# A gated matrix-memory scan on one core: its output gate by ScalarE's sigmoid two steps later instead of by exponential, addition and reciprocal, and the gate's bias added later in a step

## The reference

```
def step(carry, inp):                       # one chunk, one direction
    C, n, m = carry
    ...
    C_new = a[..., None, None] * C + einsum('bhs,bhsd,bhse->bhde', ws, kc, vc)
    w_inter = exp(inter - m_t)
    s = einsum('bhtd,bhsd->bhts', qc, kc) * exp(dmat - m_t[..., None])
    num = w_inter[..., None] * einsum('bhtd,bhde->bhte', qc, C) + einsum('bhts,bhse->bhte', s, vc)
    h = num / maximum(abs(den), exp(-m_t))[..., None]

def mlstm_readout(h, o, norm_g, w_out):     # h: forward plus backward
    hn = h * rsqrt(mean(h * h, axis=-1, keepdims=True) + EPS)
    hn = hn * norm_g
    y = hn * sigmoid(o)                     # o = x @ w_o + b_o, the output gate
    return y @ w_out
```

## Time and profile before

| | |
|---|---|
| median of 3 runs | 3857.44 us (3845.57 to 3867.3) |
| the profiled execution, its own time | 3861.1 us |
| its span | 3859.3 us |
| mean granted clock of TensorE | 0.922 |
| the scan, from step 0's L1890 to the end of the last L1951 | 2622.05 to 2917.89 us, 295.84 us |

### The profile page before, as it was taken

One profiled execution on the slowest core, in us unless ns is written; L12 is line 12 of the kernel. 1 busy time (PEld: TensorE's weight loads), 2 busy tenths in 40 slices (PEclk: granted clock), 3 DMA queues, 4 the chain that ended last, 5 costly groups with the idle time before them and its releaser, 6 DMA issues.

```text
span 3859.3 us, 37214 instructions
## 1 busy us (share of the span) xinstructions
PE 3372.9 (87%) x14970; PEld 2483.2 (64%) x14990; DVE 1545.4 (40%) x2658; ACT 839.0 (22%) x1493; POOL 745.5 (19%) x322
## 2 busy tenths in 40 slices
PE   5986888887789887999999978999977689999998
PEld 2444344444676787888888843447766668888886
DVE  3012788897342136222222334115664633222225
ACT  2013333334312212111111112101222022112111
POOL 2000000000321013332333320001111343223223
PEclk9995888888889988999999988999988889999999
DMA  5100111111112001111111130100002201111112
GB/s 141 41 22 22 55 44 44 44 44 23 55 57 96 28 23 50 44 46 52 43 54 43 44 139 28 44 25 13 13 1 93 93 22 55 44 54 44 47 51 109
DMA packets 173178, 192.25 MB, mean 50 GB/s; under 512 B 24267, under 2 KB 137803, under 8 KB 172284
## 3 DMA queue, kind: packets, MB, share of 16 engines
q1 hardware_dynamic: 163696, 177.20, 14.5%
q10 hardware_dynamic: 9356, 13.31, 1.1%
HBM read 174.71 MB, written 15.78 MB: 49 GB/s over the span
## 4 chain that ended last, share of the span: by engine, by line
PE 58%; issue 16%; DVE 15%; POOL 6%; ACT 3%; DMA 1%; ACTq 1%; POOLq 0%; SPq 0%; DVEq 0%
PE psum L605 9%; PE psum L607 9%; PE psum L606 9%; PE psum L598 7%; PE psum L588 6%; POOL weights_parts L2156 3%; PE psum L970 2%; PE psum L708 2%; DVE x_cols L1592 2%; DVE rows L1590 2%; PE psum L702 2%; POOL region L2204 2%; DVE stats L1510 1%; PE psum L746 1%; PE psum L727 1%
## 5 line engine op out<-in xcount | busy, mean ns | idle before, releaser
L2156 POOL TENSOR_TENSOR weights_parts<-weights,weights_parts 128x2048 fp32r<-128x2048 f32 (+1 forms) x82 | 377.0, 4598 | 986.9 <-ACT weights_parts L1092 986.9
L605 PE MATMUL psum<-x_cols_parts,weights_parts 128*128 128x512 f32 x1344 | 525.7, 391 | 25.6 <-POOL weights_parts L2156 23.9
L607 PE MATMUL psum<-x_cols_parts,weights_parts 128*128 128x512 f32 x1344 | 524.9, 391 | 0.0
L607 PE MATMUL psum<-weights_parts,region_parts 128*128 128x512 f32 (+1 forms) x1120 | 410.3, 366 | 0.0
L605 PE MATMUL psum<-weights_parts,region_parts 128*128 128x512 f32 x864 | 337.5, 391 | 6.9 <-DVE region_parts L2110 5.8
L606 PE MATMUL psum<-weights_parts,region_parts 128*128 128x512 f32 x864 | 337.1, 390 | 0.0
L605 PEld LDWEIGHTS psum<-x_cols_parts,weights_parts 128*128 128x128 f32 x1344 | 253.6, 189 | 79.7 <-issue 24.9
L607 PEld LDWEIGHTS psum<-x_cols_parts,weights_parts 128*128 128x128 f32 x1344 | 253.5, 189 | 53.0
L606 PE MATMUL psum<-x_rows_parts,weights_parts 128*128 128x512 f32 x704 | 275.2, 391 | 0.0
L1092 ACT ACTIVATE weights_parts<-weights 128x2048 fp32r<-128x2048 f32 (+1 forms) x82 | 155.0, 1891 | 470.0 <-DMA region<-in_bup_h_dram 142.6
L605 PE MATMUL psum<-weights_parts,x_cols_parts 128*128 128x256 f32 x768 | 222.2, 289 | 27.8 <-DVE x_rows L1694 11.7
(11 more groups left out here) (288 smaller groups left out, 5265.0 us busy)
## 6 DMA issues: line engine op xcount, KB each, us to landing
weights<-in_ada_w_dram SPq DMA_DIRECT2D x24, 1024.0 KB, 5.2
weights<-in_ffn_up_w_dram SPq DMA_DIRECT2D x44, 512.0 KB, 4.8
weights<-in_w_up_dram SPq DMA_DIRECT2D x16, 1024.0 KB, 5.1
weights<-in_w_down_dram SPq DMA_DIRECT2D x16, 1024.0 KB, 5.0
weights<-in_m_in_w_dram SPq DMA_DIRECT2D x7, 2048.0 KB, 9.0
weights<-in_ffn_down_w_dram SPq DMA_DIRECT2D x10, 1024.0 KB, 5.1
weights<-in_xa_wkv_dram SPq DMA_DIRECT2D x4, 2048.0 KB, 8.0
x_rows<-x_scratch SPq DMA_DIRECT2D x4, 2048.0 KB, 10.8
```

Source lines behind the costliest of these rows:

```text
L605: pe.matmul(o, lhsT=a_hi, rhs=b_hi, start=(first and i == 0), stop=False)
L607: m = pe.matmul(o, lhsT=a_lo, rhs=b_hi, start=False, stop=(last and i == len(terms) - 1))
L2156: pool.tensor_tensor(WLO[buf][:, 0:width], WRAW[buf][:, 0:width], WHI[buf][:, 0:width], ALU.subtract).then_inc(s("w_lo"), 1)
```

## The change

The gate's bias moves on VectorE from the end of step j to step j + 1, behind L1890 and ahead of exponents. ScalarE takes the sigmoid of the gate tiles of step j - 2 in step j, from j = 2 on, in place of exp(-o) of those of step j - 1; VectorE's addition and reciprocal go. From step 2 on ScalarE ends its step with an exponential of one column that nobody reads (warm). apply_gates waits for the sigmoid (o_sig). o_used becomes at least o_ready + 2 instead of + 1, so that heads 3 are multiplied a step later than before; five products instead of four now stand at each of the two places behind the scan.

```
+        warm = view(R, 15579, (1,))
...
         def o_used(h, m):
-            return max(10 + m, o_ready(h, m) + 1)
+            return max(10 + m, o_ready(h, m) + 2)
...
                         ins.then_inc(s("m_e"), 1)
-                        if j >= 1:
-                            gate_exp(j - 1)
+                        if j >= 2:
+                            gate_sigmoid(j - 2)
                         if j >= 10:
                             head_roots(j - 10)
+                        if j >= 2:
+                            act.activation(warm, ident[:, 0:1], ACT.Exp)
+            def gate_sigmoid(j):
                 act.wait_ge(s("o_pre"), j + 1)
                 for e in range(2):
                     v = o_slot(j // 4, 2 * (j % 4) + e)
-                    ins = act.activation(v, v, ACT.Exp, scale=-1.0)
-                ins.then_inc(s("o_exp"), 1)
+                    ins = act.activation(v, v, ACT.Sigmoid)
+                ins.then_inc(s("o_sig"), 1)
...
             scan(X_STEPS, 4, True)
-            gate_exp(15)
+            gate_sigmoid(14)
+            gate_sigmoid(15)
...
                         dve.tensor_tensor(PP[:, j % 2, :], PS[:, 1, :], DD[:, j % 2, :], ALU.mult).then_inc(s("m_pt"), 1)
+                        if j >= 1:
+                            gate_bias(j - 1)
                         if j + 1 < len(steps):
                             exponents(j + 1)
-                        if j >= 1:
-                            gate_values(j - 1)
...
                         for h in (2, 3):
                             state_step(i, d, h)
-                        gate_bias(j)
...
-            def gate_values(j):
-                dve.wait_ge(s("o_exp"), j + 1)
-                vs = [o_slot(j // 4, 2 * (j % 4) + e) for e in range(2)]
-                for v in vs:
-                    mark(dve.tensor_scalar(v, v, 1.0, None, ALU.add))
-                settled()
-                for v in vs:
-                    mark(dve.reciprocal(v, v))
...
                 if todo:
                     settled()
+                    dve.wait_ge(s("o_sig"), j - 1)
...
             scan(X_STEPS, 4, True)
+            gate_bias(15)
             head_stats(7)
-            gate_values(15)
```

More of the change, by code:

```diff
@@ L1382, in scan @@
                         ins.then_inc(s("m_e"), 1)
-                        if j >= 1:
-                            gate_exp(j - 1)
+                        if j >= 2:
+                            gate_sigmoid(j - 2)
                         if j >= 10:
                             head_roots(j - 10)
-            def gate_exp(j):
+                        if j >= 2:
+                            act.activation(warm, ident[:, 0:1], ACT.Exp)
+            def gate_sigmoid(j):
                 act.wait_ge(s("o_pre"), j + 1)
```

## The result

The changed kernel takes 3799.76 us in the median of four runs (3794.19 to 3809.75), the kernel before 3858.49 in four. The ratio is 0.9856 with a 95% interval of 0.9834 to 0.9877: faster by 1.4%. This ratio is not the quotient of the two medians, which is 0.9848. Timed again in five further runs the ratio was 0.9874 (0.9854 to 0.9895).

The account below looks back on a forecast made before the run. PE was taken to bound nine early scan steps, late DVE work the five late ones. Gains of 0.67 (step 0), 4.3 and 26.8 us, less 0.15 (last step), made 31.6: about 3826 us, range 3808 to 3838.

Parts of the forecast that it names:

- What bounds the kernel: Scan, 295.84 us: PE limits nine early steps (17.04 us each), DVE is late in five late ones (21.9 each).
- The bias: Bias behind L1890: L929's wait falls from 0.75 to some 0.08 us, a full-clock step from 15.95 to 15.28.
- Additions and reciprocals, sigmoid, late steps: 4.37 us stretch shortened, added loads in ScalarE's idle time; DVE ready at 6.0 us, late steps as long as early.
- The clock: PE in the scan's steps: lower level in four of five, 16.56 us a step, between 15.28 and 16.9.
- three gaps: PE's waits per early step: 0.57 us before the last L959, about 0.33 before L922, 0.75 before L929.
- Rival (a): Scan's steps: clock stays at 2.4 GHz once the 0.75 us gap is gone; 3808 us, chance 0.17.
- The last step: End of scan: L970 waits 0.68 us more, L1890 comes 0.66 earlier; 15.75 us instead of 15.60, +0.15.
- The range: Whole kernel: 3808 us, the end of (a), to 3838, taking in a low clock in every step plus run spread.

Follow-up runs that it names:

- sigmoid_one_late: The kernel after with the sigmoid taken for the gate of the step before instead of two steps late; ratio 0.9899.
- gate_only: The kernel after with the bias put back at the end of its step, only the gate changed; 3827.83 us, ratio 0.9933.
- exp_two_late: The kernel after with the gate again exponential, addition and reciprocal, but still two steps late; ratio 0.9881.
- bias_only: The kernel before with only the bias moved behind L1890, the gate unchanged; 3850.28 us, ratio 0.9992.
- half_bias: The kernel after with the first gate tile's bias ahead of the product of scores and decays, the second's behind; 3824.83 us in one run.
- gate_only_spread: gate_only with the second gate tile's products spread over all three places between the state products; 3802.15 us in one run.
- before_again: The kernel before, unchanged, run for a second profile; 3847.22 us in a single run.

## Why the prediction was wrong

**What bounds the kernel: right.** TensorE in the early steps, VectorE's queue behind the table loads and ahead of the reciprocals in the late ones. One reading was wrong: TensorE's matmuls have two gaps in a step, not three. The 0.33 us ahead of L922 are idle time of the weight loads (PEld), and 14.62 us of work with 0.57 and 0.75 of waiting already make the 15.95.

**The bias: right.** L1894 came 0.67 earlier, step 0 went from 17.36 to 16.72 (forecast -0.67), a step at full clock from 15.95 to 15.29 (15.28).

**Additions and reciprocals, sigmoid, late steps: right in the times, wrong in the number of loads.** VectorE ready at 6.06 (6.0), ScalarE done at 7.4 and 8.9 (7.4 and 8.9), late steps equal to early ones. 23 table loads were added, not 35 to 40 (35 start in the scan, 12 did before); none is waited for, so nothing followed from it. Even where the loads stand ahead of the next exponentials (sigmoid_one_late), late steps cost 0.95 us more (the last of them 1.7) and early ones nothing. The Trainium skill's price of 1.38 us for a drain on a switch ("ScalarE: Activation LUTs", "What ACT_TABLE_LOAD costs") is not seen here either: the load at 2677.64 is followed by its sigmoids at 2678.93, and their end by the next load at 2679.68. Its "Rules for kernel authors" would have all of one set done before a switch; here the added loads left ScalarE 9.4 us of idle time in an early step and 6.6 or more in a late one, and nothing waited for them.

**The clock: the step that failed.** "I take the lower level in four steps of five, 15.28 + 0.8 x 1.6 = 16.56, nearer to the slow end." It was none in fourteen, and the term was missed by 14 x 1.27 = 17.8 us: nine early steps gave 15.7 instead of 4.3, five late ones 33.1 instead of 26.8. The reason given was that two of three gaps stay and the stretches are packed closer. One of the two, the 0.33 us, is not a gap of the matmuls, and with the other, 0.58 us of waiting for VectorE, the clock stayed up in all fourteen steps, in three profiles. In gate_only, where only the bias stands in its old place and the wait of 0.75 us is there, it fell in nine of fourteen: with that wait gone, the low level went. Rival (a), priced at 3808 us and given 0.17, is what happened, with its condition, the 0.75 us gone: the full gain of 49.5 it promised came as 47.55.

**The last step: missed by 1.8.** Its wait of 1.93 us was forecast at about 2, but not that the clock would fall behind it: 17.55 us, forecast 15.75. That it falls is not certain either: in exp_two_late the same wait of 1.93 us was followed by 15.98 us at 1.00, and with the old wait of 1.33 the last step of before was once 15.60 at 1.00 and once 16.29 at 0.90.

**The range.** Rival (a) lay at its lower edge, and room for the spread of the runs, put at some 7 us, was added only at the upper end; what precedes the scan alone varied by some 12 us to either side. Of the 58.7 us between the first medians the scan explains 44 to 48; the other 11 to 14 lie within what the start of the scan varies from run to run, and the second comparison gave 50.9. The chances were right in their order: faster.

## What to carry to other kernels

Where a profile shows TensorE's clock falling in a regular pattern and short waits standing close together in each step, price the edit that takes one wait away at both clock levels, and give the high level its full chance: here 0.67 us of wait in a step was worth 1.75 on average in the nine early steps, of which six had been low. Two delays that stand behind each other in one in-order queue are not two terms of a sum: each alone cost about 1 us a late step here, both together (bias_only) 7.9 on average, the lower clock that came with them included. And look at every DMA queue for a small transfer on the path behind a big one that is not: moving 4 MB of copies behind 2 MB of weights gave 10 us.

## What the runs showed of the hardware

- The granted clock followed two waits of TensorE that stood close together, not one of them: with 0.57 and 0.75 us it fell in 9 of 14 steps (gate_only), with 0.58 and 0.42 in 8 of 14 (half_bias, one profile), with 0.58 alone (the kernel after) or 0.75 alone (gate_only_spread, one profile) in none, and with 0.66 and 0.57 at 3.4 us from each other in none of ten late steps (exp_two_late, sigmoid_one_late). A low step took about 1.65 us longer.
- With the same waits the pattern of one high and two low steps repeats from run to run and from kernel to kernel, 15.95 us, then two of 17.5 to 17.6; which step is the first high one differs (step 1 in before, step 2 in before_again).
- A tiny operation of VectorE is not cheap ahead of a chain: one, of one element a partition, made the gap ahead of L930 0.6 us longer (0.71 for 0.09), the second 0.07 more.
- A table load is put ahead of the activation that needs it, and may stand behind one of that activation's waits and ahead of another, as at L1375 without the small exponential. Ahead of the last gate of the kernel before it ran long before its activation:

```profile
2904.66 1.28 ACT L1393 ACT_TABLE_LOAD   x1
...
2917.92 0.72 ACT L1393 ACTIVATE extra<-extra 128x256 f32<-128x256 f32 x2 [11.98 <-DVE extra L1951]
```
